# First stage of a two-block transformer kernel: modulation tiles of the scale multiplied on TensorE, those of the shift on VectorE, with another order of the loads

## What is computed

```python
mod = silu(c) @ w_cond + b_cond                 # c: [1, 1024], w_cond: [1024, 6144]
shift_m, scale_m, gate_m, shift_f, scale_f, gate_f = split(mod, 6)
h = rmsnorm(x, g_mix_pre) * (1.0 + scale_m) + shift_m
proj = h @ w_in                                 # [512, 1024] @ [1024, 2048]
q, k, v, u = split(proj, 4)
...
x = x + gate_m * rmsnorm(mix, g_mix_post)       # then an FFN, then the second block
```

## Time and profile before

| | |
|---|---|
| median of 3 runs | 1824.24 us |
| lowest and highest | 1823.74, 1824.55 us |
| the profiled execution's own time | 1821.06 us |
| span of the profiled execution | 1819.3 us |
| TensorE busy (matmul) | 1738.4 us, 96% |
| VectorE, ScalarE, GpSimd busy | 725.6, 700.3, 787.0 us |
| mean granted TensorE clock | 0.978 |

### The profile page before, as it was taken

How to read it: one execution, slowest core, us unless ns; L and a number is a source line. 1 busy time by engine, 2 the same in 40 slices (tenths; PEclk the granted TensorE clock), 3 DMA queues, 4 the chain that set the end, 5 groups by cost and what they waited for, 6 DMA issues and landing times.

```text
span 1819.3 us, 21968 instructions
## 1 busy us (share of the span) xinstructions
PE 1738.4 (96%) x8024; PEld 1386.8 (76%) x8024; DVE 725.6 (40%) x1072; ACT 700.3 (38%) x935; POOL 787.0 (43%) x598
## 2 busy tenths in 40 slices
PE   3999998999999987999999999999999999999997
PEld 2677787888888877777777777777887788888885
DVE  5455735111110054477667757566112322222102
ACT  2554545222233334333334444445222443333332
POOL 2333244444446641534433333344444344444663
PEclk7899999999999988999999999999999999999998
DMA  8444321322223312322212222222223222222331
GB/s 330 159 143 146 121 81 54 109 92 92 92 64 100 93 56 104 104 82 72 85 64 82 70 70 81 70 80 75 100 94 128 83 98 96 92 92 72 93 90 68
DMA packets 50802, 176.34 MB, mean 97 GB/s; under 512 B 5642, under 2 KB 5898, under 8 KB 50354
## 3 DMA queue, kind: packets, MB, share of 16 engines
q1 hardware_dynamic: 50738, 175.47, 29.2%
HBM read 171.25 MB, written 4.19 MB: 96 GB/s over the span
## 4 chain that ended last, share of the span: by engine, by line
PE 90%; DVE 3%; issue 2%; ACT 2%; DMA 1%; POOL 1%; SPq 0%; DVEq 0%; POOLq 0%; ACTq 0%
PE PR L526 26%; PE PR L528 26%; PE PR L527 26%; PE AX L874 1%; DMA cond<-wcond 1%; PE AX L605 1%; PE AX L634 1%; PE AX L878 1%; PE PR L534 1%; PE AX L618 1%; PE PR L535 1%; PE PR L536 1%; DVE macc L1482 1%; PE AX L853 1%; PE PR L568 1%
## 5 line engine op out<-in xcount | busy, mean ns | idle before, releaser
L446 POOL TENSOR_TENSOR wlo<-raw,whi 128x512 fp32r<-128x512 f32 x288 | 384.6, 1335 | 953.7 <-ACT whi L957 953.5
L447 POOL TENSOR_TENSOR wlo<-raw,whi 128x512 fp32r<-128x512 f32 x288 | 398.5, 1384 | 0.0
L957 ACT ACTIVATE whi<-raw 128x1024 fp32r<-128x1024 f32 x288 | 302.2, 1050 | 170.1 <-PE PR L528 156.9
L526 PE MATMUL PR<-h3h,whi 128*128 128x512 f32 x608 | 247.8, 408 | 9.6 <-POOL wlo L447 9.6
L527 PE MATMUL PR<-h3l,whi 128*128 128x512 f32 x608 | 241.8, 398 | 0.0
L528 PE MATMUL PR<-h3h,wlo 128*128 128x512 f32 x608 | 241.6, 397 | 0.0
L526 PEld LDWEIGHTS PR<-h3h,whi 128*128 128x128 f32 x608 | 115.2, 189 | 43.2 <-issue 17.6
L526 PE MATMUL PR<-h4h,whi 128*128 128x512 f32 x352 | 140.2, 398 | 0.0
L527 PE MATMUL PR<-h4l,whi 128*128 128x512 f32 x352 | 139.4, 396 | 0.0
L528 PE MATMUL PR<-h4h,wlo 128*128 128x512 f32 x352 | 139.4, 396 | 0.0
L528 PEld LDWEIGHTS PR<-h3h,wlo 128*128 128x128 f32 x608 | 115.1, 189 | 27.8
(11 more groups left out here) (288 smaller groups left out, 3085.1 us busy)
## 6 DMA issues: line engine op xcount, KB each, us to landing
raw<-w SPq DMA_DIRECT2D x224, 512.0 KB, 3.5
cond<-wcond SPq DMA_DIRECT2D x48, 512.0 KB, 4.7
raw<-w SPq DMA_DIRECT2D x32, 384.0 KB, 3.1
raw<-w SPq DMA_DIRECT2D x32, 320.0 KB, 2.9
x<-xin SPq DMA_DIRECT2D x1, 2048.0 KB, 8.0
x_keep<-x SPq DMA_DIRECT2D x1, 2048.0 KB, 7.3
x_re<-x_keep SPq DMA_DIRECT2D x1, 2048.0 KB, 9.2
out<-outT SPq DMA_DIRECT2D x8, 256.0 KB, 2.0
```

Of the source, the lines that this page charges most:

```text
L446: pool.tensor_tensor(wlo[:, j, 0:512], raw[:, j, 0:512], whi[:, j, 0:512], ALU.subtract)
L447: pool.tensor_tensor(wlo[:, j, 512:], raw[:, j, 512:], whi[:, j, 512:], ALU.subtract).then_inc(lo_ready, 1)
L526: pe.matmul(bank, whi[:, j, w], oh[:, k0 + k, :], start=first and i == 0, stop=False)
L957: act.activation(whi[:, j, :], raw[:, j, :], ACT.Copy).then_inc(hi_ready, 1)
```

## The change

It does five things, all ahead of the second projection unit.

1. The eight tiles of the scale (8 to 15) go to TensorE directly (`mod_direct`): a 128x128 slice of the `cond` tile is the weights and the column of `cvec` the one-column moving operand, eight matmuls for a tile, added up in `PR[:, 3, 8:16]`. VectorE keeps the eight tiles of the shift. The bias is put into `PR[:, 3, 0:16]` ahead of them by one matmul with the identity.
2. The loads come in another order: vectors, constants, tiles 0, 1, 8, 2, then x, then 9, 3, 10, 4, 11, 5, 12, 6, 13, 7, 14, 15, then the weight units 0 to 3, and the attention constants and the rest behind them. The ring still has four slots, and a load waits for the use of the tile that is four places ahead of it in this order.
3. `sumsq` is cut into four pairs, which stand between the direct tiles on TensorE.
4. VectorE makes `xn` = x times the norm factor (`norm_x`) ahead of the modulation's end, between its tiles 5, 6 and 7 and behind them; the norm factor is now in PSUM (`AX[:, 1, :]`).
5. `h1h` is made on VectorE by one instruction for each k, straight from `xn`; ScalarE makes the full h in place (`full`), and the low parts follow when all of `h1h` is made. The first unit (`first_unit`) does its 8 high*high matmuls first, then 8 low*high, then 8 high*low.

```diff
+FIRST_COND = (0, 1, 8, 2, 9, 3, 10, 4, 11, 5, 12, 6, 13, 7, 14, 15)
...
+        def cond_at(n):
+            at = FIRST_COND.index(n) if n < 2 * KT else n
+            return at % RING, at // RING + 1
+
+        def cond_taken(n):
+            if n < KT:
+                return cond_used, n + 1
+            if n < 2 * KT:
+                return direct_used, n - KT + 1
+            return cond_used, n - KT + 1
...
             def load_cond(n, j):
-                if not isinstance(n, int) or n >= RING:
-                    sp.wait_ge(cond_used, n - (RING - 1))
+                if n >= 2 * KT + RING:
+                    sp.wait_ge(*cond_taken(n - RING))
+                elif n >= 2 * KT:
+                    sp.wait_ge(*cond_taken(FIRST_COND[n - RING]))
+                elif FIRST_COND.index(n) >= RING:
+                    sp.wait_ge(*cond_taken(FIRST_COND[FIRST_COND.index(n) - RING]))
...
-            sp.dma_start(vec[:, :], vecs[:, :]).then_inc(s_con, 16)
+            sp.dma_start(vec[:, :], vecs[:, :]).then_inc(s_vec, 16)
+            sp.dma_start(con[:, :], cons[:, :]).then_inc(s_con, 16)
+            for at in range(RING):
+                load_cond(FIRST_COND[at], at)
             sp.dma_start(x[:, :, :], xin[:, :, :]).then_inc(s_x, 16)
-            sp.dma_start(con[:, :], cons[:, :]).then_inc(s_con, 16)
-            sp.dma_start(att[:, :, :], atts[:, :, :]).then_inc(s_con, 16)
-            for n in range(RING):
-                load_cond(n, n)
-            with sp.Fori(0, 2) as i:
-                for j in range(RING):
-                    load_cond(RING * i + (RING + j), j)
+            for at in range(RING, 2 * KT):
+                load_cond(FIRST_COND[at], at % RING)
...
-            load_in(0)
-            for n in range(12, 16):
-                load_cond(n, n % RING)
-            for u in range(1, RING):
+            for u in range(RING):
                 load_in(u)
...
+            def mod_first():
+                for k in range(KT):
+                    mm = pe.matmul(PR[:, 3, k:k + 1], macc[:, 0, k * P:(k + 1) * P], con_("ones", 0, 1), start=False,
+                                   stop=True, skip_group_check=True)
+                mm.then_inc(msum_done, 1)
+
+            def mod_direct(n):
+                j, uses = cond_at(n)
+                pe.wait_ge(cond_in[j], 16 * uses)
+                for k in range(KT):
+                    mm = pe.matmul(PR[:, 3, KT + k:KT + k + 1], cond[:, j, k * P:(k + 1) * P], cvec[:, n - KT:n - KT + 1],
+                                   start=False, stop=True, skip_group_check=True)
+                mm.then_inc(direct_used, 1)
...
-            pe.wait_ge(s_con, 48)
-            sumsq(0)
-            mod_sum(0)
-            mod_sum(1)
+            pe.wait_ge(s_vec, 16)
+            pe.wait_ge(s_con, 16)
+            pe.matmul(PR[:, 3, 0:16], con_("ident"), vec[:, V["b_cond"]:V["b_cond"] + 16], start=True, stop=True)
+            pe.wait_ge(cvec_ready, 1)
+            mod_direct(8)
+            mod_direct(9)
+            sumsq((0, 1))
+            mod_direct(10)
+            sumsq((2, 3))
+            mod_direct(11)
+            sumsq((4, 5))
+            mod_direct(12)
+            sumsq((6, 7))
+            mod_direct(13)
+            mod_direct(14)
+            pe.wait_ge(*cond_taken(KT - 1))
+            mod_first()
+            mod_direct(15)
...
-            rms(1, sq_used, 8)
-            for u in range(LEAD):
-                hi(0, 4, u)
-            split_h(ht1, h1h, lambda k: mod[:, k:k + 1])
+            rms(1, sq_used, 8, dst=AX[:, 1, :])
+            hi(0, 4, 0)
+            for k in range(4):
+                full(k)
+            hi(0, 4, 1)
+            for k in range(4, KT):
+                full(k)
+            hi(0, 4, 2)
...
-            for n in range(16):
+            for n in range(6):
                 mod_unit(n)
-            dve.wait_ge(msum_done, 2)
-            dve.tensor_tensor(mod[:, 0:16], PR[:, 3, 0:16], cols("b_cond", 0, 16), ALU.add).then_inc(mod_ready, 1)
-            dve.wait_ge(mod_ready, 1)
-            dve.scalar_tensor_tensor(amix[:, :], mod[:, 8:16], 1.0, cols("g_mix_pre"), ALU.add, ALU.mult).then_inc(
+            dve.wait_ge(s_x, 16)
+            dve.wait_ge(r_ready, 1)
+            norm_x(0)
+            norm_x(1)
+            mod_unit(6)
+            norm_x(2)
+            norm_x(3)
+            mod_unit(7)
+            for k in range(4, KT):
+                norm_x(k)
+            dve.wait_ge(msum_done, 1)
+            dve.wait_ge(direct_used, KT)
+            dve.tensor_scalar(mod[:, 0:8], PR[:, 3, 0:8], 1.0, None, ALU.mult).then_inc(mod_ready, 1)
+            dve.scalar_tensor_tensor(amix[:, :], PR[:, 3, 8:16], 1.0, cols("g_mix_pre"), ALU.add, ALU.mult).then_inc(
                 mod_ready, 1)
             dve.wait_ge(mod_ready, 2)
-            dve.wait_ge(s_x, 16)
-            make_h(lambda k: amix[:, k:k + 1], lambda k: mod[:, k:k + 1], ht1, h1h, h1l)
+            make_h()
```

More of the change, by code:

```diff
@@ L174, in phase_a @@
                 t = dict(mix1=a("mix1", [P, KT, T], F32, s))
-            t.update(h1h=a("h1h", [P, KT, T], F32R), h1l=a("h1l", [P, KT, T], F32R), mixh=a("mixh", [P, KT, T], F32R),
+            t.update(h1h=a("h1h", [P, KT, T], F32R), h1l=a("h1l", [P, KT, T], F32R))
+            with ExitStack() as s:
+                t.update(xn=a("xn", [P, KT, T], F32, s))
+            t.update(mixh=a("mixh", [P, KT, T], F32R),
                      mixl=a("mixl", [P, KT, T], F32R), cond=a("cond", [P, RING, 1024]), macc=a("macc", [P, 2, 1024]),
@@ L468, in h_lows @@
                     pool.tensor_tensor(hl[:, k, c], hth[:, k % RING, :], hh[:, k, c], ALU.subtract).then_inc(hl_pool, 1)
-            for u in range(LEAD):
-                lo(0, u)
-            lo_parts(0, ht1, h1h, h1l)
+            lo(0, 0)
+            for k in BY_POOL:
+                lo_part_first(k)
+            lo(0, 1)
+            lo(0, 2)
             units(LEAD, U_GU1 - 1)
@@ L548, in x_sum @@
                 mm.then_inc(sqx_done, 1)
-            def sumsq(first):
-                for k in range(KT):
-                    pe.wait_ge(sq_ready, first + k + 1)
-                    mm = pe.matmul(AX[:, 0, :], con_("ones"), sq[:, k % 2, :], start=k == 0, stop=k == KT - 1)
-                    mm.then_inc(sq_used, 1)
             def sum_once(n):
@@ new lines, in sumsq, with first_unit @@
+            def sumsq(ks):
+                for k in ks:
+                    pe.wait_ge(sq_ready, k + 1)
+                    mm = pe.matmul(AX[:, 0, :], con_("ones"), sq[:, k % 2, :], start=k == 0, stop=k == KT - 1)
+                    mm.then_inc(sq_used, 1)
+            def first_unit():
+                pe.wait_ge(hi_ready, 1)
+                for k in range(KT):
+                    pe.wait_ge(hh_ready, k + 1)
+                    pe.matmul(PR[:, 0, :], whi[:, 0, k * P:(k + 1) * P], h1h[:, k, :], start=k == 0, stop=False)
+                pe.wait_ge(lo_ready, 1)
+                for k in range(KT):
+                    pe.matmul(PR[:, 0, :], wlo[:, 0, k * P:(k + 1) * P], h1h[:, k, :], start=False, stop=False)
+                for k in range(KT):
+                    pe.wait_ge(*lo_part(0, k))
+                    mm = pe.matmul(PR[:, 0, :], whi[:, 0, k * P:(k + 1) * P], h1l[:, k, :], start=False, stop=k == KT - 1)
+                mm.then_inc(unit_used, 1)
@@ L581, in in_unit @@
                     pe.wait_ge(qkvu_ready, u - 1)
-                unit(u, u % RING, h1h, h1l, 0, KT, PR[:, u % 2, :],
-                     each=(lambda k: lo_part(0, k)) if u == 0 else None)
+                unit(u, u % RING, h1h, h1l, 0, KT, PR[:, u % 2, :])
             def v_turn(p):
@@ L645, in pool_map @@
                 pe.matmul(PR[:, 2, :], wp[:, g, :], pooled[:, :], start=True, stop=True).then_inc(pooly_done, 1)
-            for u in range(3):
-                in_unit(u)
+            first_unit()
+            in_unit(1)
+            in_unit(2)
             scores(0)
@@ L964, in squares, with rms @@
                     act.activation(sq[:, k % 2, :], x[:, k, :], ACT.Square).then_inc(sq_ready, 1)
-            def rms(n, ready, count, width=D, bank=0, c=slice(0, T), load=True):
+            def rms(n, ready, count, width=D, bank=0, c=slice(0, T), load=True, dst=rr):
                 if load:
@@ L1098, in pair_high @@
                 act.activation(mixh[:, p, :], AX[:, 3, :], ACT.Copy).then_inc(mixh_ready, 1)
+            act.wait_ge(s_att, 16)
+            act.activation(late[:, :, :], att[:, :, :], ACT.Copy).then_inc(late_ready, 1)
             for u in range(3):
```

81 lines of the change are left out of this document (31 added, 50 removed).

## The result

| | before | after |
|---|---|---|
| median of 4 runs each | 1823.99 us | 1840.95 us |
| lowest and highest | 1819.54, 1824.55 | 1837.86, 1843.00 |
| the profiled execution's own time | 1821.06 | 1841.65 |
| span of the profiled execution | 1819.3 | 1839.9 |
| TensorE busy, mean granted clock | 1738.4, 0.978 | 1771.6, 0.985 |

The kernel got slower: ratio 1.0097, 95% interval 1.0075 to 1.0119, 17.0 us in the medians. The forecast was slower by 10 us (1834, range 1822 to 1838). The direction was right, the size not, and the result lies above the range.

A forecast was written before the change was run, and what follows sets the result against it. TensorE holds 90% of the span, so the start of the second unit (57.51 us) decides: +14.7 us for sums at the low clock, -4.7 us on the way to the second unit, +10.0 in all, 1834 us, range 1822 to 1838.

The forecast's parts named there:

- Loads and the first tiles: Start of the kernel: loads land in the new order, x at 15.1 us and tile 9 at 16.35.
- The clock's price: TensorE from 16.35: eight one-column groups and eight wide matmuls take 41.7 us at 1.2 GHz; sums end 14.7 us later.
- the fall at 205: Later mod_sum in the earlier trace: clock fell to 0.50 under gap-free one-column matmuls; taken as evidence for the low clock.
- the rise by a list without pauses: Rival, TensorE up to the sums: kept busy, it runs at 2.4 GHz; second unit 6.9 us earlier, 1817; chance 0.13.
- Low clock throughout: Main case, TensorE up to the sums: 1.2 GHz all along, +10.0 us, 1834; chance 0.60 without the late wait.
- the late wait: Low-clock rival: slower loads make tile 15 and weight units the last wait, +1 to +3 us more, 1837; chance 0.05.
- the rise on the way: Rival, TensorE up to the sums: a wide pair lifts the clock for a while; 1823 to 1829, middle 1827; chance 0.22.
- the wait behind the norm factor: Tile 15 and weight units wait for VectorE's tile 6, behind the norm factor; hidden by 3 us at the low clock.
- The steps from the sums to the second unit: mod, amix, h1h and low parts up to the second unit: 9.5 us instead of 14.16, 4.7 us gained.
- ScalarE's and GpSimd's shares lie beside this: Way from the sums to the second unit: extra 1 to 2 us possible only where ScalarE's step comes late.
- this cover is thin but holds: Weight units behind tile 15 land from 53 us on, still ahead of need.
- covers that fail for tiles and for ScalarE: Upper bound: covers of tiles 7 and 15 and of ScalarE failing by 1 to 4 us give 1838.

The follow-up runs named there:

- experiment 2: Changed kernel, but ScalarE and GpSimd split weight units 0 to 2 ahead of their steps for h; 1835.85 us, 1.0078 of the kernel before.
- Experiment 10: The changed kernel once more, unaltered, 12 runs; ratio 1.0063 to the kernel before.
- Experiment 3: Changed kernel with VectorE making all eight low parts and GpSimd kept out of the way to h; 1829.69 us, 1.0045 of the kernel before.
- experiment 7: Changed kernel with all sixteen tiles on VectorE, norm products between its last tiles, GpSimd idle in the way to h; 1815.84 us, 0.9977 of the kernel before.
- Experiment 5: Changed kernel with all of sumsq in one piece, behind direct tile 8 and ahead of tile 9; 1837.60 us, 1.0084 of the kernel before.
- experiment 6: Changed kernel with direct tiles' operands swapped: silu(c) column as weights, tile streamed, row of sums turned back into columns; 1833.68 us, 1.0067 of the kernel before.

## Why the prediction was right or wrong

*Loads and the first tiles: right within a microsecond.* Tile 9 was forecast for 16.35 and its group began at 16.79.

*The clock's price: right.* Eight groups of 3.5 us and pairs of 3.4, and the sums at 58.05; measured 57.91. Choosing the fall at 205 over the rise by a list without pauses was the right choice for this execution, and the trace of experiment 2 shows the fall by itself, in the midst of one-column work. The Trainium skill's advice in "TensorE: Matmul & The Clock Gate", section "Why this matters for your kernels", to keep TensorE continuously busy, isn't borne out here: from 16.79 to 57.91 it was busy without a gap, at 1.2 GHz.

*The clock's chance: too sure.* "Low clock throughout" had 0.65 with and without the late wait, the rise on the way 0.22. Experiment 10 has seven runs of twelve in the faster group, and I take these for the rise, on the strength of the one profile; those of experiments 2 and 3, with the same list up to the sums, show it too (sums at 47.9 and 49.2). The first four runs, 1837.9 to 1843.0, all lay near the slower group, which was chance. Over the twelve runs of experiment 10 the changed kernel is 11.5 us slower than the one before (1.0063, from 6.6 to 16.4 us), close to the 10 of the forecast, and that would have been luck: a clock that rises in about half of the executions takes off what the way to h adds. The forecast's size of the rise was fair (sums 48.96, within its 46.5 to 53), and the wait behind the norm factor that it named did become real there, at 2.78 us. It wasn't in the low case, as the sum had it: tiles 7 and 15 came hidden.

*The steps from the sums to the second unit: wrong, and this is the step that failed.* "VectorE ends `h1h` at 1.15 + 8 x 0.49 = 5.1 us and the six low parts at 0.69 at 9.2". Measured behind the sums: `h1h` ends at 7.0, the low parts at 16.1. By its terms: `mod` and `amix` were 0.8 us shorter than put (the 0.94 of `amix` in the earlier trace rows was itself measured beside GpSimd, see the last section), `h1h` 2.7 longer, the low parts 5.0 longer, the rest 0.3: +7.2 us, and with it 16.7 instead of 9.5. This is the whole miss of the medians, 1840.95 against 1834: in the profiled execution the clock stayed low, as the forecast took it, and the other three have times like it. The durations were taken from rows where GpSimd wasn't in the way, and "ScalarE's and GpSimd's shares lie beside this" was the sentence that hid the cost. Experiment 3 gives 10.1 with GpSimd away, so the price of the forecast was right and its condition wasn't met.

*Why GpSimd was there.* In the kernel before, GpSimd had split all three weight units by 44.5 us. The new order loads the weight units behind tile 15, and the new lists split units 1 to 3 beside the steps of h (63.19 to 73.42), the second of which TensorE first wants at 74.61. The forecast saw the first ("this cover is thin but holds") and counted only when TensorE would need the weights, not what making them does to VectorE. The trace of before had the warning. GpSimd, then VectorE, timelines of the kernel before:

```profile
33.61 2.25 POOL L447 TENSOR_TENSOR wlo<-raw,whi 128x512 fp32r<-128x512 f32 x1
...
40.80 1.26 POOL L447 TENSOR_TENSOR wlo<-raw,whi 128x512 fp32r<-128x512 f32 x1
```

```profile
29.69 1.28 DVE L1482 SCALAR_TENSOR_TENSOR macc<-cond,cvec,macc 128x1024 f32<-128x1024 f32 x1 [1.60 <-DMA cond<-wcond]
32.48 7.23 DVE L1482 SCALAR_TENSOR_TENSOR macc<-cond,cvec,macc 128x1024 f32<-128x1024 f32 x4 [1.51 <-DMA cond<-wcond]
```

The same `wlo` takes 2.25 us at 33.61 and 1.26 at 40.80. Of the four tiles on VectorE from 32.48 on, the two beside GpSimd's work take 2.25 and 2.10 us, the other two 1.29 and 1.28.

*The rule that I didn't weigh.* What the runs show: with both engines at work VectorE's 0.47 us (3.74 for eight in experiment 7) becomes 1.41 from one `h1h` to the next, its 0.61 (4.90 for eight) becomes 1.69 from one low part to the next, and GpSimd's 1.26 becomes up to 1.72. The two take turns. GpSimd and VectorE, single instructions of the kernel after:

```profile
70.02 1.72 POOL L466 TENSOR_TENSOR wlo<-raw,whi 128x512 fp32r<-128x512 f32 x1
70.53 1.76 DVE L1485 TENSOR_TENSOR h1l<-xn,h1h 128x512 fp32r<-128x512 f32 x1
71.70 1.72 POOL L467 TENSOR_TENSOR wlo<-raw,whi 128x512 fp32r<-128x512 f32 x1
```

They end at 71.74, 72.29 and 73.42. From 60.5 to 74.0 us, where both engines have work, GpSimd's instruction always ends 1.13 to 1.15 us after VectorE's, and VectorE's ends 0.28 us (`h1h`) or 0.54 to 0.56 us (low part) after GpSimd's.

The Trainium skill has this rule and it speaks against the change: "SBUF — State Buffer", section "SBUF: two separate sides", calls the port pair that the two share an exclusive lock, which whichever starts first holds for its whole instruction while the other blocks. The trace agrees: the ends alternate at these fixed distances, as they would if one engine's work began when the other's had ended.

*The bounds.* 1838 took in covers that fail for tiles and for ScalarE, "1 to 4 us". It had no term for two engines that hold each other up.

## What to carry to other kernels

A duration belongs to the neighbours it was measured with: before taking one from a group of rows, look at what the engine that shares its memory ports does at that moment, and at what it will do in the new order. Work that is moved to hide it can still cost where it lands, here 7 us by GpSimd's work beside VectorE, most of it the splitting of weights that nobody was waiting for yet. And count a matmul by the clock that its width leaves: one column for each set of weights did no more for the clock here than idling does, so move such sums to TensorE only where it would be idle and isn't waited for, or stream the large operand past a narrow weight.

## What the hardware showed that I hadn't expected

- The same list of instructions gave two groups of times, 1826.5 to 1831.6 and 1839.6 to 1845.4 us, and two traces of it differ in whether the clock rises behind the first pair of wide matmuls (3.76 us in both): at 25.4 us, or not before 70. A list near that edge has no single time. Experiment 5, with the wide matmuls in one piece, had its four runs within 4.3 us, but so had the first four runs of the changed kernel within 5.2, so four can't tell.
- Weights of one column and 512 moving columns held the clock as full weights do: 1.88 us for two float32 matmuls of 512 columns (experiment 6).
- `amix` took 0.16 us where it had taken 0.94, 0.8 us that no one had counted. In the kernel before, GpSimd was at work beside it:

```profile
43.25 1.26 POOL L447 TENSOR_TENSOR wlo<-raw,whi 128x512 fp32r<-128x512 f32 x1
```

  This ended at 44.51, and `amix`, with both sources in SBUF, at 44.53; `mod`, with one source in PSUM, had taken 0.17 us beside the same instruction. After the change `amix` reads one source from PSUM, and GpSimd was idle at that moment; in experiment 2 it took 0.15 us (48.06) beside a GpSimd instruction that ran from 47.01 to 48.28. So the 0.94 was mostly a wait for GpSimd's turn to end, and in these rows an instruction with a source in PSUM doesn't have that wait. No run was made for this alone.
